# Post-norm turns with the squares as the stationary operand, the norm weight at eviction and the residual added two tiles at a time

## The reference

```python
def rms_norm_2(x, g):
    xf = x.astype(jnp.float32)
    y = xf * lax.rsqrt(jnp.mean(xf * xf, axis=-1, keepdims=True) + NORM_EPS)
    return (y * g.astype(jnp.float32)).astype(x.dtype)

# the second block's loop, DEPTH = 2, SEQ = 256, D_MODEL = 1024
    for i in range(DEPTH):
        ...
        if i % 2 == 0:
            h = rms_norm_2(x, ev_pre_g[j])
            h = even_mixer(h, ...)
            x = x + rms_norm_2(h, ev_post_g[j])
        else:
            h = rms_norm_2(x, od_pre_g[j])
            h = odd_mixer(h, od_w_in[j], od_w_out[j])
            x = x + rms_norm_2(h, od_post_g[j])
        h = conv_ffn(rms_norm_2(x, ffn_pre_g[i]), ffn_w_up[i], ffn_conv_w[i], ffn_conv_b[i], ffn_w_down[i])
        x = x + rms_norm_2(h, ffn_post_g[i])
```

## Time and profile before

| | us |
|---|---|
| median of three runs | 1796.07 (1795.59 to 1799.13) |
| the profiled execution's own time | 1789.62 |
| its span, first to last instruction | 1787.8 |
| mean granted TensorE clock | 0.981 |
| PE busy / DVE busy / ACT busy | 94% / 69% / 53% of the span |

### The profile page before, as it was taken

The page is one execution under the profiler, slowest core; times in us unless marked ns, Lnnn a source line. Parts: engine busy times, 40 slices in busy tenths (PEclk is TensorE's granted clock), DMA queues, the critical chain, the costliest instruction groups (busy, mean ns, idle before and its releaser), DMA issues.

```text
span 1787.8 us, 29027 instructions
## 1 busy us (share of the span) xinstructions
PE 1675.5 (94%) x10712; PEld 1498.2 (84%) x10712; DVE 1234.8 (69%) x2021; ACT 943.9 (53%) x1638; POOL 14.1 (1%) x20
## 2 busy tenths in 40 slices
PE   6999999899999999997999999878999999879997
PEld 5888897698888888886888889777999787779986
DVE  6666766567776777666677766757777566478765
ACT  5555453555555555455565545356665443366652
POOL 1000000000000000000000000000000000000000
PEclk9999999899999999998999999999999999999998
DMA  7454553255546554550355456204554553145442
GB/s 277 165 188 158 196 201 119 82 177 192 191 154 215 189 188 153 203 176 21 104 209 188 152 178 233 95 24 177 189 179 145 192 195 113 42 147 177 167 163 88
DMA packets 47361, 286.13 MB, mean 160 GB/s; under 512 B 5996, under 2 KB 6764, under 8 KB 23968
## 3 DMA queue, kind: packets, MB, share of 16 engines
q1 hardware_dynamic: 44640, 278.94, 44.4%
q10 hardware_dynamic: 2240, 5.19, 0.8%
q0 software_dynamic: 384, 0.68, 0.1%
HBM read 283.74 MB, written 1.05 MB: 159 GB/s over the span
## 4 chain that ended last, share of the span: by engine, by line
PE 86%; DVE 8%; ACT 4%; issue 1%; DMA 0%; ACTq 0%; SPq 0%; DVEq 0%
PE ps_gemm L129 33%; PE ps_gemm L137 15%; PE ps_gemm L140 15%; PE ps_gemm L139 8%; PE ps_gemm L138 8%; DVE s_wlo L89 3%; ACT s_whi L80 1%; PE ps_s L791 1%; PE ps_gemm L791 1%; PE ps_gemm L816 1%; PE ps_sum L192 1%; PE ps_sum L816 1%; ACT s_work L838 1%; DMA s_wraw<-in_stream_dram 0%; PE ps_sum L744 0%
## 5 line engine op out<-in xcount | busy, mean ns | idle before, releaser
L89 DVE TENSOR_TENSOR s_wlo<-s_wraw,s_whi 128x1024 fp32r<-128x1024 f32 (+3 forms) x608 | 630.3, 1078 | 408.7 <-ACT s_whi L80 408.6
L80 ACT ACTIVATE s_whi<-s_wraw 128x1024 fp32r<-128x1024 f32 (+3 forms) x608 | 540.2, 936 | 413.4 <-PE ps_gemm L140 204.3
L129 PE MATMUL ps_gemm<-s_xr,s_whi 128*128 128x256 f32 x2192 | 402.8, 286 | 11.7 <-DVE s_xr L253 8.9
L129 PEld LDWEIGHTS ps_gemm<-s_xr,s_whi 128*128 128x128 f32 x2192 | 344.5, 193 | 17.5 <-issue 11.8
L129 PE MATMUL ps_gemm<-s_xr,s_wlo 128*128 128x256 f32 x1096 | 311.0, 284 | 0.0
L137 PE MATMUL ps_gemm<-s_xr,s_whi 128*128 128x512 f32 x704 | 277.9, 396 | 4.9 <-DVE s_mem_v L698 3.1
L140 PE MATMUL ps_gemm<-s_xr,s_whi 128*128 128x512 f32 x704 | 277.7, 396 | 0.0
L129 PEld LDWEIGHTS ps_gemm<-s_xr,s_wlo 128*128 128x128 f32 x1096 | 211.3, 193 | 0.0
L137 PE MATMUL ps_gemm<-hid_r,s_whi 128*128 128x512 f32 x528 | 208.1, 394 | 0.0
L140 PE MATMUL ps_gemm<-hid_r,s_whi 128*128 128x512 f32 x528 | 208.0, 394 | 0.0
L139 PE MATMUL ps_gemm<-s_xr,s_wlo 128*128 128x256 f32 x704 | 196.6, 279 | 0.0
(11 more groups left out here) (346 smaller groups left out, 2169.0 us busy)
## 6 DMA issues: line engine op xcount, KB each, us to landing
s_wraw<-in_stream_dram SPq DMA_DIRECT2D x178, 1024.0 KB, 4.8
s_wraw<-in_stream_dram SPq DMA_DIRECT2D x96, 704.0 KB, 4.0
s_wraw<-in_stream_dram SPq DMA_DIRECT2D x16, 768.0 KB, 4.3
s_wraw<-in_stream_dram SPq DMA_DIRECT2D x14, 512.0 KB, 3.3
s_room<-in_o_bias_dram ACTq DMA_DIRECT2D x1, 1536.0 KB, 9.6
s_room<-in_mem_dram SPq DMA_DIRECT2D x4, 256.0 KB, 4.7
s_x<-in_x_dram SPq DMA_DIRECT2D x1, 1024.0 KB, 5.0
s_room<-in_e_alibi_dram ACTq DMA_DIRECT2D x1, 1024.0 KB, 5.9
```

Of the source, the lines that this page charges most:

```text
L80: c.act.activation(c.whi[:, slot, s], c.wraw[:, raw, s], ACT.Copy).then_inc(c.hi_ready, 1)
L89: last = c.dve.tensor_tensor(c.wlo[:, slot, s], c.wraw[:, raw, s], c.whi[:, slot, s].bitcast(F32), ALU.subtract)
L129: last = pe.matmul(out, a, b, start=start and i == 0, stop=stop and i == 2, skip_group_check=skip)
```

## The change

It rewrites the four turns.

- Square and sum: ACT squares the mixers' output straight from PSUM. The squares are the stationary operand and one column of `mean_d` moves (`token_sums_pe`), so that sums over features come out as two columns, one for each 128 tokens, in `ps_t`. The last tile's square goes to PE directly and is not added into `c.acc`.
- Inverse: Ln and Exp on 128x2 into `c.inv_col`; `spread_pe` then makes PE multiply each column, broadcast to 128x128, with the identity, so that the inverse stands on all partitions of `ps_sum`. DVE reads it from there. In mix_o this spread lies between the two tiles of unit 1 and ACT copies it to `c.inv`; the two transposes are gone.
- The post-norm weight is multiplied in when a tile is evicted (mixers) or by one more `tensor_scalar` for each tile (convolution stages), no longer in the scaling.
- Scaling, addition and the second squares go by groups of one or two tiles (`POST_GROUPS`), with the group's squares in `c.sq2` or `c.hsq` by turns. Before mix_o ACT rounds residual times weight directly, and DVE writes the rest with one instruction.
- Splits: after the mixers the first half of the coming stage's first rest lies ahead of the last eviction and the second behind it; after the convolution stages the whole lies ahead of the last tile. ACT's rounding of the next unit is done in halves.
- The output is stored in four parts, each as its group is added.

The core of the diff (helpers with the same body elsewhere are cut):

```diff
+POST_GROUPS = {"norm": ((0, 2), (2, 2), (4, 2), (6, 1), (7, 1)), "late": ((0, 1), (1, 1), (2, 2), (4, 2), (6, 2)),
+               "out": ((0, 2), (2, 2), (4, 2), (6, 2))}
+def token_sums_pe(c, sq, first, last):
+    for i in range(sq.shape[1] // P):
+        tt = i % 2
+        ins = c.pe.matmul(c.ps_t[:, tt:tt + 1], sq[:, i * P:(i + 1) * P], c.mean_d[:, 0:1],
+                          start=first and i == 0, stop=last and i >= sq.shape[1] // P - 2, skip_group_check=True)
+    return ins
+def spread_pe(c, cnt, cols, done):
+    cnt.inv += 1
+    c.pe.wait_ge(c.t_inv, cnt.inv)
+    for tt in range(2):
+        last = c.pe.matmul(c.ps_sum[:, cols + tt * P:cols + (tt + 1) * P], c.inv_col[:, tt:tt + 1].to_broadcast([P, P]),
+                           c.ident[:, :], start=True, stop=True)
+    last.then_inc(done, 1)
...
+def post_norm_pe(c, cnt, kind):
+    c.pe.wait_ge(c.sq_added, cnt.sq + KD - 1)
+    token_sums_pe(c, c.acc, True, False)
+    c.pe.wait_ge(c.sq_ready, cnt.sq + KD)
+    token_sums_pe(c, c.sq[:, (KD - 1) % 2, :], False, True).then_inc(c.sq_added, 1)
+    cnt.sq += KD
+    spread_pe(c, cnt, 0, c.t_spread)
+    if kind == "norm":
+        for g in range(len(POST_GROUPS[kind])):
+            group_sums_pe(c, cnt, POST_GROUPS[kind], g)
+        cnt.group += len(POST_GROUPS[kind])
+        spread_pe(c, cnt, T, c.t_spread)
...
+def post_norm_act(c, cnt, kind, gain):
+    c.act.wait_ge(c.sq_added, cnt.sq)
+    token_inverse_act(c, cnt)
+    if kind == "out":
+        return
+    groups, u = POST_GROUPS[kind], cnt.split
+    split_hi_half(c, u, 0)
+    if kind == "norm":
+        split_hi_half(c, u, 1)
+    for g, (first, n) in enumerate(groups):
+        c.act.wait_ge(c.post_added, cnt.post + g + 1)
+        if kind == "late":
+            for k in range(first, first + n):
+                c.act.activation(c.xhi[:, k, :], c.x[:, k, :], ACT.Identity,
+                                 scale=c.gains[:, gain + k:gain + k + 1]).then_inc(c.xhi_ready, 1)
+        if g >= 2:
+            c.act.wait_ge(c.t_summed, cnt.group + g - 1)
+        c.act.activation(group_buffer(c, g)[:, 0:n * T], c.x2[:, first * T:(first + n) * T], ACT.Square).then_inc(c.t_sq, 1)
+        if kind == "late" and first + n == KD // 2:
+            split_hi_half(c, u, 1)
+    cnt.split += 1
+    cnt.post += len(groups)
+    cnt.group += len(groups)
+    c.act.wait_ge(c.t_summed, cnt.group)
+    token_inverse_act(c, cnt)
+    if kind == "late":
+        cnt.xn += KD
+        cnt.unscaled += KD
+        c.act.wait_ge(c.sum_done, cnt.norm + 1)
+        c.act.activation(c.inv[:, :], c.ps_sum[:, 0:T], ACT.Copy).then_inc(c.inv_ready, 1)
+        cnt.norm += 1
+def post_norm_dve(c, cnt, kind, gain, half=False):
+    if half:
+        split_lo_half(c, cnt.split, 1)
+        cnt.split += 1
+    groups = POST_GROUPS[kind]
+    cnt.spread += 1
+    c.dve.wait_ge(c.t_spread, cnt.spread)
+    def wide(v, g):
+        first, n = groups[g]
+        return v[:, first:first + n, :]
+    def scaled(g):
+        both = c.ps_sum[:, 0:T].unsqueeze(1).to_broadcast([P, groups[g][1], T])
+        c.dve.tensor_tensor(wide(c.xn, g), wide(c.xn, g), both, ALU.mult).then_inc(c.post_scaled, 1)
+    def added(g):
+        c.dve.wait_ge(c.post_scaled, cnt.post + g + 1)
+        c.dve.tensor_tensor(wide(c.x, g), wide(c.x, g), wide(c.xn, g), ALU.add).then_inc(c.post_added, 1)
+    def rests(g):
+        first, n = groups[g]
+        for k in range(first, first + n):
+            c.dve.wait_ge(c.xhi_ready, cnt.xn + k + 1)
+            c.dve.scalar_tensor_tensor(c.xlo[:, k, :], c.x[:, k, :], c.gains[:, gain + k:gain + k + 1],
+                                       c.xhi[:, k, :].bitcast(F32), ALU.mult, ALU.subtract).then_inc(c.xlo_ready, 1)
+    for g in range(len(groups) + 2):
+        if g < len(groups):
+            scaled(g)
+        if 0 < g <= len(groups):
+            added(g - 1)
+        if kind == "late" and g > 1:
+            rests(g - 2)
+    if kind == "late":
+        cnt.xn += KD
+        cnt.unscaled += KD
+    cnt.post += len(groups)
+    split_below(split_lo, c, cnt, cnt.split + 1)
...
-        for half in range(n == 0, 2 if n < KD - 1 else 1 if conv is None else 0):
+        for half in range(n == 0, 2 if n < KD - 1 else 1):
...
-def post_norm_dve(c, cnt, gain, ahead=None):
-    split_below(split_lo, c, cnt, cnt.split + 1)
-    inverse_dve(c, cnt)
-    for k in range(KD + (2 if ahead is not None else 1)):
-        if k < KD:
-            c.dve.scalar_tensor_tensor(c.xn[:, k, :], c.xn[:, k, :], c.gains[:, gain + k:gain + k + 1],
-                                       c.inv[:, :], ALU.mult, ALU.mult).then_inc(c.post_scaled, 1)
-        if 0 < k <= KD:
-            c.dve.wait_ge(c.post_scaled, KD * cnt.post + k)
-            c.dve.tensor_tensor(c.x[:, k - 1, :], c.x[:, k - 1, :], c.xn[:, k - 1, :], ALU.add).then_inc(c.post_added, 1)
-            if ahead is not None:
-                c.dve.wait_ge(c.post_added, KD * cnt.post + k)
-                ahead_dve(c, ahead, k - 1, None)
-        if ahead is not None and 1 < k <= KD + 1:
-            ahead_lo_dve(c, cnt, k - 2, None, 0)
-    if ahead is not None:
-        cnt.xn += KD
-    split_below(split_lo, c, cnt, cnt.split + 1)
-    cnt.post += 1
-    cnt.sq += KD
-def post_norm_act(c, cnt, ahead=False):
-    inverse_act(c, cnt)
-    if cnt.post == 3:
-        return
-    split_below(split_hi, c, cnt, cnt.split + 1)
-    all_squares_act(c, cnt, c.x, c.post_added, KD * cnt.post + 1, ahead=ahead)
-    cnt.post += 1
...
+        split_below(split_lo, c, cnt, min(u + 3, last + 1) if post is not None else u + 3 if u < last else u + 2)
+        if post is not None and u == last:
+            split_lo_half(c, last + 1, 0)
         c.dve.wait_ge(c.unit_done, u + 1)
         bank = bank_of(c, cnt.out)[:, 0:wide * T]
         s = slice(n * T, (n + wide) * T)
-        if post:
-            ins = c.dve.tensor_copy(c.xn2[:, s], bank)
-        else:
-            ins = c.dve.tensor_tensor(c.x2[:, s], c.x2[:, s], bank, ALU.add)
-        ins.then_inc(c.bank_free, 1)
+        if post is not None:
+            c.dve.wait_ge(c.sq_ready, cnt.sq + n + wide)
+            for k in range(n, n + wide):
+                ins = c.dve.tensor_scalar(c.xn2[:, k * T:(k + 1) * T], bank[:, (k - n) * T:(k - n + 1) * T],
+                                          c.gains[:, post + k:post + k + 1], None, ALU.mult)
+            ins.then_inc(c.bank_free, 1)
+            for k in range(n, min(n + wide, KD - 1)):
+                add_squares(c, cnt, k, k == 0, 0)
+            cnt.out += 1
+            continue
+        c.dve.tensor_tensor(c.x2[:, s], c.x2[:, s], bank, ALU.add).then_inc(c.bank_free, 1)
         cnt.out += 1
         for k in range(n, n + wide):
             if ahead is not None:
...
+    def spread_inverse():
+        spread_pe(c, cnt, 0, c.sum_done)
+        cnt.norm += 1
+        cnt.group += len(POST_GROUPS["late"])
     for i in range(8):
         feature_tiles_pe(c, cnt, u0 + i, 2, KD, c.xhi, c.xlo, (c.xlo_ready, cnt.xn + 1) if i == 0 else None, late=True,
-                         tile_sums=i == 0)
-        if i == 1:
-            inverse_columns_pe(c, cnt)
+                         groups=POST_GROUPS["late"] if i == 0 else None, between=spread_inverse if i == 1 else None)
         if i == 2:
             pe.wait_ge(c.bank_free, g0 + 2)
...
-            sp.wait_ge(c.post_added, 4 * KD)
-            sp.dma_start(h["out"], c.x).then_inc(c.out_stored, 16)
-            sp.wait_ge(c.out_stored, 16)
+            stored = sum(len(POST_GROUPS[kind]) for kind in ("norm", "late", "norm"))
+            for g, (first, n) in enumerate(POST_GROUPS["out"]):
+                sp.wait_ge(c.post_added, stored + g + 1)
+                sp.dma_start(h["out"][:, first:first + n, :], c.x[:, first:first + n, :]).then_inc(c.out_stored, 16)
+            sp.wait_ge(c.out_stored, 16 * len(POST_GROUPS["out"]))
```

More of the change, by code:

```diff
@@ L43 @@
 OUT_TILES = {12: 1, 8: 1, 4: 2}
+AFTER = {"mix_e": "norm", "conv_0": "late", "mix_o": "norm", "conv_1": "out"}
 LATE_SCALED = ("mix_a", "ffn2_0", "ffn1_1", "mix_b", "ffn2_1", "mix_e", "mix_o")
@@ L289, in ffn_pe @@
     per = 2 if wide else 1
-    if name != "ffn1_0" and not late:
-        for k in range(KD):
-            norm_sums_pe(c, cnt, k)
     def up(j, turn):
@@ L532, in ffn_dve @@
             ahead_dve(c, ahead, n, None)
-        add_squares(c, cnt, n, n == 0, 0)
+        if conv is None or n < KD - 1:
+            add_squares(c, cnt, n, n == 0, 0)
+        else:
+            dve.wait_ge(c.sq_ready, cnt.sq + KD)
         if ahead is not None:
             ahead_lo_dve(c, cnt, n, None, 0)
+        if conv is not None:
+            dve.tensor_scalar(c.xn2[:, s], c.xn2[:, s], c.gains[:, post + n:post + n + 1], None, ALU.mult).then_inc(c.post_gained, 1)
+    if conv is not None:
+        cnt.gained += KD
+        dve.wait_ge(c.post_gained, cnt.gained)
     cnt.ffn += 1
@@ L538, in ffn_dve @@
     cnt.sq += KD
```

(12 more changed lines are left out.)

138 lines of the change are left out of this document (75 added, 63 removed).

## The result

The changed kernel takes 1804.2 us (median of 14 runs, 1800.1 to 1806.8), the one before, beside it, 1793.2 (14 runs, 1788.8 to 1800.2). The ratio is 1.0057, 95% interval 1.0046 to 1.0068: slower by some 10 us, near the upper end of the stated range. The forecast case (+3.1) did not come; the rival "clearly slower" (1806) did. The profiled execution of the change took 1805.8 (span 1804.0), that of the kernel before 1789.6.

The account below looks back on a forecast made before the run. TensorE, busy 94%, was taken to bound the kernel through its idle time and clock. Turn 1 +1.7, turn 2 +0.7, turn 3 +3.2 and end -2.5 gave +3.1 on 1796.1, so 1799.2 us; range 1791 to 1806.

Parts of the forecast that it names:

- The forecast case: Whole kernel: slow first products and a later turn 3 outweigh the shorter end, +3.1 us to 1799.2; chance 0.52.
- clearly slower: Sums at 0.21 us per instruction at low clock, chain 11.4 for 9.24, whole 1806 us; chance 0.14.
- The bound: Whole kernel: TensorE busy 94%, so time changes only where PE stands still or runs at a lower clock.
- The price of a one-column sum: Norm sums in the turns: 0.14 us per instruction at the low clock, range 0.11 to 0.21.
- First products at the low clock: Start of conv_0 and conv_1: products run at 1.2 GHz, 2.0 us lost each, bounds 1.0 to 2.8.
- Turn 3: From mix_o to conv_1: scaling starts 1.2 us later, first products lose 2.0, together +3.2.
- Turn 2 and mix_o: After conv_0: earlier scaling and products, then a new wait; +0.7 us, or +2.0 if the clock stays low longer.
- The new wait: Before mix_o's unit 2: ACT and DVE wait for the inverse spread within unit 1; start 1450.9 for 1450.3, +0.7.
- The end: After conv_1: earlier scaling 0.3, paired instructions 0.8, smaller last store 1.4; -2.5 us, range -1.1 to -3.3.
- The clock is no worse: Turns: loads of 128 columns count as work, so the clock returns in the sums; 1794 us, chance 0.20 including another rival.
- faster: Turns: cheap loads, sums follow the adds at full clock, second halves 7.7 for 9.24; 1791 us, chance 0.14.
- the change doesn't do what it says: Turns: their waits are hidden elsewhere, only the end counts; 1793.5 us, chance counted within another rival's 0.20.

Follow-up runs that it names:

- the four remedies: Changed kernel with sums moving 128 columns, half split behind evictions, mix_o's unit 2 split before the wait, constant matmuls in idle stretches: 1784.21 us, ratio 0.9951.
- the early split: Changed kernel with mix_o's unit 2 split on ACT and DVE ahead of the wait for the spread inverse: 1799.63 us, ratio 1.0028 to the kernel before.
- the old sums: Changed kernel with only the second norm's sums after mix_e and mix_o put back to 256 moving columns: 1799.02 us, ratio 1.0031 to the kernel before.
- fillers alone: Changed kernel plus constant matmuls into an unread bank, in PE's idle stretches and between sum groups: 1791.52 us, ratio 0.9984 to the kernel before.

## Why the prediction was right or wrong

**The bound** was right: PE's clock and idle time decided. All of the difference but the 2.7 us ahead of turn 1 lies in the four turns, the first products behind them and mix_o.

**The price of a one-column sum** is the step that failed: "I take 0.14, the middle of 0.11 and 0.17, as one column moves". It is 0.216 at the low clock and 0.11 at the full one, and with 128 moving columns hardly more (0.23 at the low clock), so nearly the whole price is the load of 128 columns, and it follows PE's clock. I had 0.21 as the far bound and took the middle without a row for it; the row of 0.17 was of two loads by themselves. The rule named there, of the Trainium skill, "TensorE: Matmul & The Clock Gate", section "LDWEIGHTS (loading the stationary operand)" (columns / 1.2 in ns, so by estimate 107 ns for 128 columns, no term for the gate), agrees with the 0.11 at full clock and not with the 0.216; the measurement decides. That a price of 0.21 gives a chain of 11.4 was worked out rightly: measured 11.43. The sum for 0.14 was not: 32 instructions of 0.14 from 2.65 on end at 7.1, and I name no wait that makes it 7.7, so by my own price the chain was some 0.5 shorter than the 9.3 that I wrote. Turn 1's first scaling came 0.4 sooner, for the 0.3 forecast; but up to the first product the turn was to be shorter by 0.3 and was longer by 1.8.

**First products at the low clock** were right in mechanism and size: 2.0 for each of conv_0 and conv_1, measured 1.9 and 2.4. The run with 128 moving columns gave conv_0's 1.9 back, for the reason named: what the sums had done for the clock was in their moving columns. Of conv_1's 2.4 it gave back 1.2.

**Turn 3** was right in kind and too small: first scaling +1.2 forecast, +2.1 measured. The order of the half split is 1.3 of it (6.36 for 7.63 without it). The rest is PE's eight sums and the spread at the low clock: from the first sum, 1584.25, to the first scaling, 1587.96, are 3.7, for the 2.8 of my sum. With the old order and the full clock of the four remedies the first scaling comes 5.95 after the last product. Turn 3 with conv_1 is +6.7 for +3.2.

**Turn 2 and mix_o** were the costliest miss: +0.7, or +2.0, forecast; +6.2 measured in the profile. The turn itself did better than before, as worked out (first scaling 0.6 sooner, products 2.57 behind it). The new wait was named, but its chain was longer: unit 2 starts 27.6 after conv_0's last product for 24.5 before, +3.2. Unit 0's sums and products ran slow for longer (the first of the three windows above, 10.4, where the earlier trace rows has 1431.7 to 1436.2), and ACT's two DMA issues took 1.23 between the copy and the rounding where I had 0.5 for both. The remaining 3.0 us are two further slow stretches (unit 2 and what follows up to unit 3 take 11.9 for 10.4, and a later gap between products 8.8 for 7.2). They come in some executions and not in others (mix_o 142.2 and 142.1 in the two profiles of the change, 138.8 and 138.1 in two experiments that left mix_o's code as changed). That the early split gives back 4 to 5 us by the medians shows the wait as a cause; how often each stretch comes I can't tell.

**The end** was right: -2.5 forecast, -3.0 measured. The store gave 1.9 for my 1.4 and the paired instructions 1.0 for 0.8; the first scaling 0.14 sooner for 0.3.

**Against the medians.** The forecast was put on 1796.1, the median of three runs; 14 runs gave 1793.2. So the miss in the difference (+3.1 for 10 to 11) is larger than the miss in the time (1799.2 for 1804.2). That 1804.2 lies in the range of 1791 to 1806 is in part luck: the range reached to the far rival, and the base was 2.9 too high. About 1793.2 the same range ends at 1803. The rival that came had the price of 0.21, chain 11.4, turns +4 and +6 (measured +3.6 and +6.7) and 1806; I gave it a chance of 0.14, for a middle price that no row supported. Its turn 2 was too small by 4 (+2 for +6.2 with mix_o). "The clock is no worse" fell with the rows at 0.50 over the sums, and "faster" with it, since it needed full clock there; "the change doesn't do what it says" fell with each turn moving by its own mechanism.

**What is shown and what is not.** Shown: the one moving column keeps the clock low (the same loads with 128 columns, -8.5, and with the old sums full clock at conv_0 again); the clock is the larger part of the loss (the same code with and without fillers, 7 to 8; fillers alone, -12.5, though the clock still fell in the chain; with the sums, the wait and the order mended too, -18 to -20); the wait in mix_o costs. Not shown: why 128 moving columns bring the clock back early in turn 1 and late in turn 3, and what sets off the two later slow stretches of mix_o, since they stand behind waits in some executions and not behind the same waits in others.

## What to carry to other kernels

Before turning a matmul round so that fewer columns move, ask what its moving columns did for the clock: here the new instructions cost about the same as the old ones at full clock, and yet left what stood behind them at half speed. Where PE stands idle in a turn, constant matmuls into a spare bank hold the clock, if they stand in the idle time and not in the chain; but look first at who sets the chain, since where DVE does they buy nothing. A store in pieces at a kernel's end is the cheapest gain of the whole change. And compare profiles only after subtracting what comes by chance: two executions with the same code in mix_o differed by 3.4 us there.
